# Gate and up products of a decoder's feed-forward with seven block products in place of eight

## The reference

```python
def ffn_half(x, g, wg, wu, wd):
    return x + 0.5 * swiglu(rms_norm(x, g), wg, wu, wd)

def swiglu(h, wg, wu, wd):
    return (jax.nn.silu(h @ wg) * (h @ wu)) @ wd

x = ffn_half(x, g_ffn1, w1_gate, w1_up, w1_down)
... # u = rms_norm(x); projection, windowed attention, pooling, memory attention, merge
x = x + merge(...)
x = ffn_half(x, g_ffn2, w2_gate, w2_up, w2_down)
y = rms_norm(x, g_final)
```

## Time and profile before

| | |
|---|---|
| median of 3 runs | 2605.3 us (2605.16 to 2605.95) |
| profiled execution | 2608.5 us, its span 2606.8 us |
| TensorE, VectorE, ScalarE, GpSimd busy | 97%, 48%, 21%, 5% |
| first FFN, first matmul to the next stage's first | 35.7 to 800.7 us |
| second FFN, first to last matmul | 1830.9 to 2584.6 us |
| mean granted TensorE clock | 0.982 |

### The profile page before, as it was taken

How to read it: one execution, slowest core, us unless ns; L and a number is a source line. 1 busy time by engine, 2 the same in 40 slices (tenths; PEclk the granted TensorE clock), 3 DMA queues, 4 the chain that set the end, 5 groups by cost and what they waited for, 6 DMA issues and landing times. The chain is left out here.

```text
span 2606.8 us, 39024 instructions
## 1 busy us (share of the span) xinstructions
PE 2523.9 (97%) x15959; PEld 2476.7 (95%) x15959; DVE 1239.1 (48%) x2248; ACT 557.6 (21%) x1056; POOL 129.0 (5%) x192
## 2 busy tenths in 40 slices
PE   7999999999998999999899799999899999999998
PEld 6999999999997899999899799989899999999997
DVE  6444444444454363444455534342644444444444
ACT  5111111111123232333322212132311111111112
POOL 0000000000011110001201100002000000000000
PEclk8999999999999998999999989999999999999999
DMA  4111111111002532112432612101211111111101
GB/s 165 34 47 48 48 48 48 48 48 48 32 1 83 189 122 83 46 60 70 119 126 88 170 57 106 41 33 49 81 49 48 48 48 48 48 48 48 48 0 74
DMA packets 108498, 172.66 MB, mean 66 GB/s; under 512 B 4822, under 2 KB 90070, under 8 KB 108025
## 3 DMA queue, kind: packets, MB, share of 16 engines
q1 hardware_dynamic: 95384, 119.33, 14.0%
q0 software_dynamic: 13024, 52.07, 6.1%
HBM read 149.79 MB, written 21.59 MB: 66 GB/s over the span
## 5 line engine op out<-in xcount | busy, mean ns | idle before, releaser
L437 PE MATMUL ps<-uh,stream_high 128*128 128x352 f32 (+1 forms) x2448 | 804.0, 328 | 23.6 <-DVEq L2034 9.1
L438 PE MATMUL ps<-uh,stream_low 128*128 128x352 f32 (+1 forms) x2448 | 791.5, 323 | 0.0
L439 PE MATMUL ps<-ul,stream_high 128*128 128x352 f32 (+1 forms) x2448 | 787.5, 322 | 0.0
L437 PEld LDWEIGHTS ps<-uh,stream_high 128*128 128x128 f32 x2448 | 467.3, 191 | 33.1 <-issue 24.5
L438 PEld LDWEIGHTS ps<-uh,stream_low 128*128 128x128 f32 x2448 | 467.0, 191 | 1.7 <-issue 1.0
L439 PEld LDWEIGHTS ps<-ul,stream_high 128*128 128x128 f32 x2448 | 467.5, 191 | 0.0
L437 PE MATMUL ps<-uh,ffn_up_h 128*128 128x352 f32 (+1 forms) x1056 | 338.8, 321 | 5.3 <-DVE ffn_up_l L582 5.3
L437 PE MATMUL ps<-ffn_hid_h,ffn_d_h 128*128 128x352 f32 (+1 forms) x1056 | 339.6, 322 | 3.3 <-DVE x L627 3.3
L438 PE MATMUL ps<-ffn_hid_h,ffn_d_l 128*128 128x352 f32 (+1 forms) x1056 | 340.1, 322 | 0.0
L439 PE MATMUL ps<-ffn_hid_l,ffn_d_h 128*128 128x352 f32 (+1 forms) x1056 | 338.4, 320 | 0.0
L438 PE MATMUL ps<-uh,ffn_up_l 128*128 128x352 f32 (+1 forms) x1056 | 338.0, 320 | 0.0
(11 more groups left out here) (277 smaller groups left out, 2446.7 us busy)
## 6 DMA issues: line engine op xcount, KB each, us to landing
stream_raw<-in_w_in SPq DMA_DIRECT2D x25, 1024.0 KB, 5.3
stream_raw<-in_w_gate SPq DMA_DIRECT2D x22, 1024.0 KB, 5.2
ffn_raw_up<-in_w_up SPq DMA_DIRECT2D x22, 1024.0 KB, 7.2
ffn_raw_d<-in_w_down SPq DMA_DIRECT2D x22, 1024.0 KB, 4.8
front_beside<-in_cache_mem_kv POOLq DMA_DIRECT2D x16, 512.0 KB, 4.8
outer<-in_cache_win_kv POOLq DMA_DIRECT2D x6, 1024.0 KB
x_kept<-x POOLq DMA_DIRECT2D x1, 4128.0 KB, 19.1
outer<-x_kept POOLq DMA_DIRECT2D x1, 4128.0 KB, 12.5
```

What stands on the lines that cost most here:

```text
L437: pe.matmul(out, w_high, a_high, start=first, stop=False)
L438: pe.matmul(out, w_low, a_high, start=False, stop=False)
L439: return pe.matmul(out, w_high, a_low, start=False, stop=last)
```

## The change

Both weights are now multiplied in blocks. For a *side* (gate or up) of a pair, the weights are a 2 x 2 block matrix: 2 halves of the contraction (4 tiles each, `K2`) by 2 hidden tiles. x is 2 halves of the contraction by 2 halves of the tokens (516 columns, `HALF`). The 2 x 2 by 2 x 2 block product takes seven products of combined blocks. The tokens of a half are again cut in two (`QW` = 258 columns), j = 0 and 1. So a side is two *groups* (j) of seven products, each 4 k x 3 matmuls of 258 columns into one bank; a group uses four banks, and the next group the other four.

- `Lefts`: weight combinations. Each side loads 1 MB (one buffer). GpSimd makes four sums of 512 elements, ScalarE seven high parts of 512 from raw or sums, VectorE seven low parts. The tile of product n for the next side is overwritten when that product of group j = 1 is done, and the block after that is loaded when all seven are split.
- `Rights`: combinations of x times gain, made once per FFN for each j and kept in SBUF: per j two gain multiplications of 1032 elements and three differences on VectorE, one difference on GpSimd, eight scaled copies of 258 and seven high parts of 1032 on ScalarE, seven low parts of 1032 on VectorE. Those of j = 1 are made between the steps of side 0, group 0. They take the place of the parts that load_tokens, blend and `Rest` made.
- Four results from accumulated banks: products 1, 6, 7 and 4 add up in one bank, in this order, and ScalarE copies the bank after 1, 6 and 7 (`copy`); TensorE waits for the copy before it adds the next product there (`copied`). VectorE adds the other banks to the copies and multiplies with rstd (gate) or with the gated values (up): `take`, three additions and four multiplications a group.
- Silu runs on ScalarE in gate sides, two at steps 4 and 6 of the group and two at the next group's step 0; GpSimd multiplies with rstd (`gate`). In GpSimd's program the four gates of j = 0 stand ahead of the next side's sums.
- The hidden tiles go to memory in fp32. When all 22 are there, a second phase (`Down`) goes over 3 chunks x 22 hidden tiles: each step loads 1 row of weight tiles (512 KB) and a chunk of the hidden tile, splits both, and does 8 outputs x 3 matmuls into eight banks that stay accumulating over the chunk's 22 steps. The down weights are read three times. x is updated once per output tile and chunk, not 11 times.
- All loops over sides and steps are written out; `Fori` is gone from the FFN. The first FFN's norm work is done one tile per down step, and at its end TensorE makes all three means; all three roots and reciprocals go to the next stage (`Rest(..., 0)`).
- ScalarE, VectorE and GpSimd wait at the first FFN's start for the bias table's transfer (`m.bias_stored`).

```diff
@@ load_tokens, blend @@
-            def high(c, half):
-                act.wait_ge(taken, 2 * 3)
-                for k in range(4 * half, 4 * half + 4):
-                    parts.scalar_high(act, k, c)
...
-            for t in range(2):
-                m.stream.split_low(dve, 0, t)
...
-    return Rest(parts, 1)
@@ ffn @@
+ORDER = (1, 2, 6, 5, 7, 3, 4)
+BANK = {1: 0, 6: 0, 7: 0, 4: 0, 2: 1, 5: 2, 3: 3}
+FRESH = (1, 2, 5, 3)
+TAKES = 8
...
+class Rights:
...
+    def scalar_steps(self, act, j):
+        self.scalar_gained(act, 4, 1, 0, j)
+        act.wait_ge(self.gained, 2 * j + 1)
+        self.scalar_high(act, 1, 5, j)
+        yield
+        act.wait_ge(self.gained_act, 2 * K2 * j + K2)
+        self.scalar_high(act, 2, 4, j)
+        yield
+        self.scalar_gained(act, 3, 1, 1, j)
+        act.wait_ge(self.combined, 3 * j + 2)
+        self.scalar_high(act, 6, 6, j)
+        yield
...
+    def vector_steps(self, dve, j):
+        self.vector_gained(dve, 5, 0, 0, j)
+        self.vector_gained(dve, 7, 0, 1, j)
+        self.vector_low(dve, 1, 5, j)
+        yield
...
+        self.difference(dve, 5, 7, 5, j, self.combined)
+        self.vector_low(dve, 2, 4, j)
+        yield
...
+        self.difference(dve, 6, 3, 5, j, self.combined)
...
+        self.difference(dve, 4, 4, 6, j, self.combined)
...
+        self.vector_low(dve, 6, 6, j)
+        yield
...
+class Lefts:
...
+    def gpsimd(self, gp, q):
+        self.arrived(gp, q)
+        if q:
+            gp.wait_ge(self.ready, len(ORDER) * q)
+        gp.tensor_tensor(self.sum(0), self.block(1, 0), self.block(1, 1), ALU.add).then_inc(self.made, 1)
+        gp.tensor_tensor(self.sum(2), self.block(0, 0), self.block(1, 0), ALU.subtract).then_inc(self.made, 1)
...
+    def scalar(self, act, q, n, product_done):
+        p = ORDER[n]
...
+        if p in S_ORDER:
+            act.wait_ge(self.made, 4 * q + S_ORDER[p] + 1)
+        if q:
+            act.wait_ge(product_done, 2 * len(ORDER) * q - len(ORDER) + n + 1)
+        act.activation(self.tiles[0][p - 1], self.source(p), ACT.Copy).then_inc(self.rounded, 1)
...
+class Down:
...
+    def tensor(self, pe, s, taken):
+        c, f = divmod(s, FT)
+        pe.wait_ge(self.ready, s + 1)
+        for o in range(KD):
...
+            if f == 0 and c:
+                pe.wait_ge(self.added, (c - 1) * KD + o + 1)
+            last = product(pe, self.m.ps[:, o, width(c)], self.d_h[:, s % 2, o * P:(o + 1) * P],
...
@@ ffn, TensorE @@
-            with pe.Fori(0, LAST) as i:
-                pair(i, False)
-            pair(LAST, True)
+            def one(q, j, n):
+                g, p = group(q, j), ORDER[n]
+                if j == 0:
+                    pe.wait_ge(lefts.ready, ALL * q + n + 1)
+                if q == 0:
+                    pe.wait_ge(rights.low_done, ALL * j + n + 1)
+                if n == 0 and g >= 2:
+                    pe.wait_ge(taken, TAKES * (g - 1))
+                if BANK[p] == 0 and n:
+                    pe.wait_ge(copied, 3 * g + n // 2)
...
+                for k in range(K2):
+                    first, last = k == 0 and p in FRESH, k == K2 - 1
+                    pe.matmul(out, w_h[:, k, :], a_h[:, k, :], start=first, stop=False, skip_group_check=True)
+                    pe.matmul(out, w_l[:, k, :], a_h[:, k, :], start=False, stop=False, skip_group_check=True)
+                    end = pe.matmul(out, w_h[:, k, :], a_l[:, k, :], start=False, stop=last, skip_group_check=True)
@@ ffn, ScalarE @@
+            def after(q, j, n):
+                if n in (0, 2, 4):
+                    copy(q, j, n // 2)
+                if n == 0 and group(q, j) and (group(q, j) - 1) // 2 % 2 == 0:
+                    for late in (2, 3):
+                        silu((group(q, j) - 1) // 4, 1 - j, late)
+                if q % 2 == 0 and n in (4, 6):
+                    silu(q // 2, j, n // 2 - 2)
+                if j and q + 1 < SIDES:
+                    lefts.scalar(act, q + 1, n, product_done)
...
@@ ffn, VectorE @@
+                    for n in range(ALL):
+                        take(q, j, n)
+                        if prepare:
+                            next(prepare)
+                        if j and q + 1 < SIDES:
+                            lefts.vector(dve, q + 1, n)
...
@@ ffn, GpSimd @@
+            for q in range(SIDES):
+                if q % 2 == 0:
+                    for n in range(4):
+                        gate(q // 2, 0, n)
+                if q + 1 < SIDES:
+                    lefts.gpsimd(gp, q + 1)
+                if q % 2 == 0:
+                    for n in range(4):
+                        gate(q // 2, 1, n)
```

More of the change, by code:

```diff
@@ L535, in _ @@
+            for q in range(SIDES):
+                for j in range(2):
+                    if rest and group(q, j) == 1:
+                        rest.tensor(pe, NCH - 1)
+                    for n in range(ALL):
+                        one(q, j, n)
+            for s in range(DOWN_STEPS):
+                down.tensor(pe, s, taken)
             if norm:
-                norm.tensor_mean(pe, NCH - 1, DOWN_UNITS)
+                for c in range(NCH):
+                    pe.wait_ge(down.added, LATE + norm.banks[c] + 1)
+                    norm.tensor_mean(pe, c, (c + 1) * KD)
@@ L565, in _, with copy @@
-            with act.Fori(0, LAST) as i:
-                pair(i, True)
-            pair(LAST, False)
-            if norm:
-                for n in range(DOWN_UNITS):
-                    c, o = divmod(n, KD)
-                    act.wait_ge(down_added, LAST * DOWN_UNITS + (n + 5))
-                    norm.scalar_square(act, n, n % 2, m.x[:, o, chunk(c)], c)
-                    if n < LATE:
-                        norm.parts.scalar_high(act, o, c)
-                    if c == 1 and o == 6:
-                        norm.scalar_root(act, 0)
+            def copy(q, j, n):
+                g = group(q, j)
+                act.wait_ge(product_done, done(q, j, 2 * n))
+                if g:
+                    act.wait_ge(taken, TAKES * (g - 1) + (3, 7, 5)[n])
+                act.activation(part[:, n, :], bank(g, 1), ACT.Copy).then_inc(copied, 1)
@@ new lines, in normed @@
+            def normed(n):
+                c, o = divmod(n, KD)
+                act.wait_ge(down.added, n + 1)
+                norm.scalar_square(act, n, n % 2, m.x[:, o, chunk(c)], c)
+                if n < LATE:
+                    norm.parts.scalar_high(act, o, c)
+            for s in range(2, DOWN_STEPS):
+                c, f = divmod(s, FT)
+                down.scalar(act, s)
+                if then is not None and s in (6, 8):
+                    act.wait_ge(product_done, done(SIDES - 1, 1, ALL - 1))
+                    stream.split_high(act, stream.base, s // 2 - 3)
+                if norm and c and 2 <= f < 2 + KD:
+                    normed((c - 1) * KD + f - 2)
@@ new lines, in _ @@
+            down.vector(dve, 1)
+            for s in range(2, DOWN_STEPS):
+                c, f = divmod(s, FT)
+                down.vector(dve, s)
+                if then is not None and s in (6, 8):
+                    stream.split_low(dve, stream.base, s // 2 - 3)
+                if f == 0:
+                    for o in range(KD):
+                        down.add(dve, (c - 1) * KD + o)
+                if norm and c and 2 <= f < 2 + KD:
+                    n = (c - 1) * KD + f - 2
+                    norm.parts.vector_low(dve, n + 1, f - 2, c - 1)
@@ L813, in vector_start, with vector_pair @@
         dve.sem_inc(self.taken, self.banks)
-    def vector_pair(self, dve, i, take, after=None, before=None):
+    def vector_pair(self, dve, i, take, after=None, before=None, more=True):
         for n in range(2 * NCH):
```

544 lines of the change are left out of this document (352 added, 192 removed).

## The result

The changed kernel takes 2575.4 us, the median of four runs (2573.1 to 2577.4); the kernel before, beside it on the same chip, 2605.2. The ratio is 0.9885, with a 95% interval from 0.9873 to 0.9898: 29.9 us faster. Forecast were 2591.8, 13.5 us faster, in a range from 2545 to 2630. So the side was right and the size less than half of what came. The profiled execution took 2577.4 us.

A forecast was written before the change was run, and what follows sets the result against it. TensorE was taken as the bound. Matmuls -115.9, first sides +73.6, gate sides +46, earlier losses -21.5, starts -6.2, chunk changes +3, first FFN's tail +7.5 sum to -13.5 us: 2591.8 us median, range 2545 to 2630.

The forecast's parts named there:

- The line through two widths: Gate and up matmuls: spacings at 352 and 328 columns give 0.45 ns a column and 2.4 ns fixed.
- The rivals of 110 and of 123.6 ns: Gate and up: a 258-column matmul costs 110 ns (2525 us, chance 0.05) or 123.6 ns (2626 us, chance 0.12).
- the term of +46: Gate sides: TensorE waits for the seventh product's bank in the second group, 2.3 us a pair over 20 pairs.
- The backlog: Gate sides: VectorE behind, so ScalarE late to the next side's first copy; 0.2 to 0.6 us more a pair.
- The cheap rival: Preparation: engines don't lock, ScalarE's order costs 1.0 us a pair, the first side 48 us; 2548 us, chance 0.20.
- the 6.7 us added for it: First side: GpSimd's lock lengthens VectorE's 19.2 us of first-token-group preparation by 6.7 us, to 25.9.
- Losses of before: Start and end losses of the earlier kernel's two FFNs, 16.4 and 5.1 us, go away: -21.5 us.
- The two changes of chunk: Down phase: eight adds of 0.44 us delay the next low parts, 1.5 us an FFN, +3 in all.
- the half clock: First sides: TensorE's 1.2 GHz level while starved, priced at nothing beyond the upper end.
- The slower rivals: Matmuls of 123.6 ns (2626 us, chance 0.12), longer gate-side chain (2636, 0.18), down steps waiting (2631, 0.03).
- the chain growing to 4.5 us: Gate sides: GpSimd to ScalarE chain costs 4.5 us, +44: 2636 us, chance 0.18; against: TensorE's gap lets others catch up.
- The 104 ns: Matmul spacing with a 128x128 weight load each, read from eight 64-column matmuls; it had to fit under 118 ns.

The follow-up runs named there:

- experiment 6: Changed kernel with gate and up matmuls, save each bank's first, cut to 200 columns: 2565.6 us; to 128: 3209.5; to 128 from the eleventh side: 2913.1.
- Experiment 2: Changed kernel with VectorE making only 1 of 128 columns of each weight low part from the second side on: 2553.4 us, ratio 0.9793.
- experiment 4: Changed kernel with ScalarE's copies of finished banks moved between the preparation steps in each FFN's first side: 2579.0 us, ratio 0.9903.

## Why the prediction was right in its direction and short in its size

**The matmuls: right within 1%.** Forecast 119.0 ns; within a product the gaps average 119.8, and a pair without losses takes 40.27 us, not 39.98. Over 21 sides of each FFN that is +6.1 us. The line through two widths held at 258 columns and not below: at 200 and 128 it gives 92 and 60 ns, and 111 came (experiment 6). The rivals of 110 and of 123.6 ns fell. To 110 also leads the rule of the Trainium skill ("TensorE: Matmul & The Clock Gate", back-to-back issue gap), which the page gives for an isolated matmul and not for a stream in which each matmul loads its weights; at 200 and 128 columns it would give 86 and 56 ns, against the 111 measured.

**The gate sides: the step that failed.** The place, the engine and the order of the chain were forecast. What failed is the price of TensorE's wait there, the term of +46: 2.3 us a pair were forecast and 1.51 measured, +30 in all, so -15.8 us over 20 pairs. It came about in three parts. Counted from the side's start at 270.19, the third sum was to end at 18.9 and ended at 18.44. The copy was to end at 20.5 and ended at 19.9: two high parts back to back take 1.15 us, not 1.2, and the copy begins before they have ended. TensorE wanted the bank at 18.7, not 18.5. So 2.1 became 1.25. The backlog, which I had at 0.2 more, was 0.26, and most of it was what I had named, ScalarE's late copy in the next side. A term of 46 us that is the difference of two numbers near 19 had to be worked to a tenth; I rounded each link up by one or two.

**GpSimd and VectorE lock each other: shown.** Experiment 2 takes VectorE's part away and the sums fall from 1.74 to 1.29 us. The Trainium skill said so in "SBUF — State Buffer", two separate sides, and the trace agrees. The cheap rival (2548 us), which needed the lock not to be there, is out: the preparation did cost what I said, and a gate side 1.51 and not 1.0.

**The first sides: right.** 53.6 and 59.4 for 54.5 and 59.1, and the links came as well: VectorE ended the first token group 24.9 us after the start (25.9 forecast), ScalarE reached the copy for the second group's third product at 42.2 (42.8). The 19.2 us of VectorE's work come to 18.0 by the two figures beside them, so the lock cost more than the 6.7 us added for it, and the two slips offset each other in part. That ScalarE's walk through the steps in order sets the length is borne out by experiment 4, where the first sides shrank by 4.0 and 5.2 us. What the account lacked is the side behind: there the sums, late behind the gates, took all of it back.

**Losses of before, tails, starts: right, and a little better.** The start came 2.7 us earlier than forecast. The end of the first FFN, from its last down matmul (770.03) to the next stage, is 6.7 us. Down products take 159.4 ns, not 161.6, which is most of the 6.6 us by which the two down stages are shorter; I had carried a row of a mixed stretch over to a pure one. The two changes of chunk took 0.2 and 0.4 us of waiting, not 1.5 an FFN.

**The sum.** Stalls -15.8, spacing +6.1 (without the first sides), two costs that were not in the sum +2.9, down and tail -6.6, start -2.7, first sides -0.6, front and blend +1.9: -14.8, as in the table. The +2.9 are the hand-over from the last gate and up product to the first down product (0.9 in each FFN, 0.7 of it the wait for its low part) and 1.1 us behind the first side of the second FFN. I had priced the half clock at nothing, as TensorE is starved there anyway; it outlasted the starved side, and the first product behind it took 2.58 us in place of 1.44:

```profile
1865.60:1868.40 2.80, 2.80 (x15) 2.80 (x14) 2.80 (x7) 0.94 (x2) 1.00 (x1) 0.50 0.00 0
```

That the spacing and the down stages nearly cancel is luck. The sum of -13.5 was the small difference of -116 and about +100, so one term wrong by a third doubled it. The slower rivals had half of their weight on the chain growing to 4.5 us; it did not grow, because TensorE's own gap resets it in each pair, as the point against it said: in the trace the gap before the seventh product is 1.09 us in each gate side from 165 to 499 us.

## What to carry to other kernels

When the bound engine gets less to do (here 12% of gate and up), look at the first instruction of another engine that stands in program order before what the bound engine needs next, and ask whether that work has a later deadline. Here 80 gates without haste stood before the sums, and turning the two round was worth as much as the whole change (28 us). A wait's name tells who was late, not what sets the length: moving the copy that the 8.8 us gap named shortened its side by 4 to 5 us, and the side behind gave all of it back. With the sums ahead of all gates and one product moved off VectorE, 6 us came.

## What the runs showed of the hardware that I had not expected

At full clock the matmuls with their 128x128 weight loads started 111 ns apart, whether they moved 200 or 128 columns. The 104 ns that the prediction read from the earlier trace rows at 64 columns was too low: the first of the eight starts lies close to the second, and from the second on, seven matmuls take 0.94 us, with one of them 0.28 long, so their starts are 110 ns apart too.

```profile
1032.07 0.94 PE L1175 MATMUL ps<-front_beside 128*128 128x64 f32 x7
```

So of the 119.8 ns at 258 columns only 9 could still be saved by narrower tiles.

Shorter matmuls made the kernel 634 us slower than the changed one (3209.5 for 2575.4), because TensorE went on at its 1.2 GHz level through both gate and up phases, although from 100 to 640 us it was never idle. In the changed kernel the granted clock was 0.71 and 0.67 in the two starved first sides and 1.00 in the rest of gate and up and in the down phases, with gaps of 1.1 us every 42 us; with 200 columns, from 100 to 500 us, it was 0.95 to 0.97. A tiling into 128-column products would have needed this run before anything else.
